# A PEER expert layer: 64 latent tokens instead of 32 fetched by gathers, 448 instead of 480 token columns in the dense expert products

## What is computed

```python
q = (xb @ w_pq).reshape(TOK_BLOCK, PEER_HEADS, 2, D_KEY_HALF)          # 8 heads, 2 halves
s = jnp.einsum('thcd,hcnd->thcn', q, sub_keys)                         # 128 keys a half
s1, i1 = lax.top_k(s[:, :, 0], 16); s2, i2 = lax.top_k(s[:, :, 1], 16)
top_s, pos = lax.top_k(s1[..., :, None] + s2[..., None, :], 16)        # 16 of 16 x 16
eidx = ...   # i1 * 128 + i2 of the chosen: 128 picks a token out of 16384 experts
g = jax.nn.softmax(top_s)
a = jax.nn.gelu(jnp.einsum('thkd,td->thk', u_exp[eidx], xb))
out = jnp.einsum('thk,thkd->td', g * a, v_exp[eidx])
```

## Time and profile before

| | us |
|---|---|
| three executions: median (lowest to highest) | 3987.83 (3984.5 to 3989.89) |
| profiled execution: its time | 3981.41 |
| profiled execution: span from first to last instruction | 3979.6 |
| u stage, layer 0 and 1 | 785.8 and 782.9 |
| v stage, layer 0 and 1 | 667.1 and 668.8 |

### The profile page before, as it was taken

How to read it: one execution, slowest core, us unless ns; L and a number is a source line. 1 busy time by engine, 2 the same in 40 slices (tenths; PEclk the granted TensorE clock), 3 DMA queues, 4 the chain that set the end, 5 groups by cost and what they waited for, 6 DMA issues and landing times.

```text
span 3979.6 us, 57585 instructions
## 1 busy us (share of the span) xinstructions
PE 3838.0 (96%) x21170; PEld 3355.6 (84%) x21170; DVE 2916.1 (73%) x4499; ACT 1673.6 (42%) x2920; POOL 2279.5 (57%) x1240
## 2 busy tenths in 40 slices
PE   7978899999999999999989989999999999999998
PEld 5756898888888888888879989888888888888886
DVE  4775218899875499999983320889987549999997
ACT  3265323556666422223231131355666643222322
POOL 1101224666666688888842222467666668888884
PEclk8999999999999999999999999999999999999999
DMA  5302324788888899999954312378888889999995
GB/s 209 129 2 81 127 85 138 264 281 305 302 302 308 313 342 317 330 319 327 335 181 175 117 54 90 131 257 285 300 302 300 311 314 341 314 327 322 321 333 185
DMA packets 396808, 972.44 MB, mean 244 GB/s; under 512 B 32160, under 2 KB 221344, under 8 KB 382880
## 3 DMA queue, kind: packets, MB, share of 16 engines
q1 hardware_dynamic: 301664, 630.72, 46.9%
q0 software_dynamic: 92160, 335.59, 22.7%
q10 hardware_dynamic: 2752, 3.21, 0.2%
HBM read 835.37 MB, written 133.96 MB: 244 GB/s over the span
## 4 chain that ended last, share of the span: by engine, by line
PE 57%; issue 26%; POOL 12%; DVE 4%; DMA 1%; DVEq 1%; ACT 0%; POOLq 0%; ACTq 0%
PE PS L775 30%; PE PS L763 18%; PE PS L565 5%; POOL SL L445 5%; POOL ROWS L452 4%; POOL SL L436 3%; PE PS L755 3%; DVE ROWS L1262 1%; PE PS L716 1%; DVE OH L1251 1%; DMA ROWS<-u_exp,EI 1%; DVE PO L1188 0%; DVE TS L1183 0%; DVE ABF L1218 0%; PE PS L548 0%
## 5 line engine op out<-in xcount | busy, mean ns | idle before, releaser
L445 POOL TENSOR_TENSOR SL<-RW,SH 128x1024 fp32r<-128x1024 f32 x512 | 1333.2, 2604 | 728.6 <-ACT SH L989 715.4
L989 ACT CAST SH<-RW 128x1024 fp32r<-128x1024 f32 x512 | 537.2, 1049 | 1430.3 <-PE PS L775 826.5
L763 PE MATMUL PS<-HH,SH 128*128 128x480 f32 x2048 | 799.6, 390 | 5.5 <-POOL SL L445 4.2
L775 PE MATMUL PS<-WH,SH 128*128 128x480 f32 x2048 | 777.0, 379 | 2.2 <-ACT GE L995 1.3
L763 PE MATMUL PS<-HH,SL 128*128 128x480 f32 x2048 | 776.5, 379 | 0.0
L763 PE MATMUL PS<-HL,SH 128*128 128x480 f32 x2048 | 776.3, 379 | 0.0
L775 PE MATMUL PS<-WH,SL 128*128 128x480 f32 x2048 | 775.2, 379 | 0.0
L775 PE MATMUL PS<-WL,SH 128*128 128x480 f32 x2048 | 775.1, 378 | 0.0
L436 POOL TENSOR_TENSOR SL<-RW,SH 128x1024 fp32r<-128x1024 f32 x84 | 202.6, 2416 | 808.3 <-ACT SH L820 808.3
L1312 DVE TENSOR_TENSOR WL<-GL,WH 128x480 fp32r<-128x480 f32 x256 | 558.6, 2182 | 20.6 <-ACT WH L1028 17.4
L1251 DVE TENSOR_TENSOR OH<-PS,PK 128x1024 f32<-128x1024 f32 x240 | 291.5, 1220 | 221.7 <-PE PS L755 207.7
(11 more groups left out here) (171 smaller groups left out, 5225.5 us busy)
## 6 DMA issues: line engine op xcount, KB each, us to landing
RW<-u_blk SPq DMA_DIRECT2D x256, 512.0 KB, 4.5
RW<-v_blk SPq DMA_DIRECT2D x256, 512.0 KB, 5.9
gate_acts<-GE SPq DMA_DIRECT2D x256, 240.0 KB, 3.2
router_weights<-GT SPq DMA_DIRECT2D x60, 1024.0 KB, 5.0
GB<-router_weights SPq DMA_DIRECT2D x32, 1920.0 KB, 14.5
GL<-gate_acts SPq DMA_DIRECT2D x256, 240.0 KB, 5.5
RW<-wstream SPq DMA_DIRECT2D x100, 512.0 KB, 4.3
AW<-wpairs SPq DMA_DIRECT2D x40, 1024.0 KB, 4.9
```

Source lines behind the costliest of these rows:

```text
L445: nc.gpsimd.tensor_tensor(SL[:, r % 2], RW[:, r % RAW], SH[:, r % 2].bitcast(F32), ALU.subtract).then_inc(raw_used, 1)
L763: last = mm(PS[:, n % 2, NG:NS], w[:, n % 2, j], a[:, j, NG:NS], start=(j == 0 and q == 0), stop=(j == DJ - 1 and q == 2))
L775: last = mm(PS[:, dj, NG:NS], w[:, k % 2, dj], a[:, k, NG:NS], start=start, stop=stop)
L989: nc.scalar.copy(SH[:, r % 2], RW[:, r % RAW]).then_inc(hi_done, 1)
```

## The change

`NG` goes from 32 to 64. From it follow `ND` 480 to 448 (columns of every dense product), `NQ` 120 to 112, `NTG` 30 to 28 (the groups of 16 tokens in the stores and loads of gate weights), `GQ` 4 to 2 picks side by side, `PG` 32 to 64 and `NPICK` 160 to 192. The table `PICK_AT` spreads the 32 more gathers of `u_exp` over the same blocks. `FOLD` gets 64 columns of its own in the constants.

```diff
-NG = 32
+NG = 64
 ND = NS - NG
 GQ = P // NG
 PG = PICKS // GQ
 NPICK = PICKS + PG
...
-PICK_AT = (_spread(20, 28, 9) + _spread(28, 45, 21) + _spread(45, 68, 36) + _spread(68, 91, 36)
-           + _spread(91, 127, NPICK - 102))
+PICK_AT = (_spread(20, 28, 11) + _spread(28, 45, 27) + _spread(45, 68, 42) + _spread(68, 91, 42)
+           + _spread(91, 127, NPICK - 122))
 VPICK_AT = _spread(2, NB_E, NPICK)
-C_MEAN, C_HEAD, C_SWAP, C_ID, C_IOTA, C_SEL, C_COS, C_SIN = 0, 128, 256, 384, 512, 640, 672, 1184
-C_ALL = 1696
+C_MEAN, C_HEAD, C_SWAP, C_ID, C_IOTA, C_SEL, C_FOLD, C_COS, C_SIN = 0, 128, 256, 384, 512, 640, 648, 712, 1224
+C_ALL = 1736
...
-    FOLD = CO[:, C_SEL:C_SEL + NG]
+    FOLD = CO[:, C_FOLD:C_FOLD + NG]
...
-    for s in range(32):
+    for s in range(2):
         c[:, C_SEL + s] = p % 32 == s
+    for t in range(NG):
+        c[:, C_FOLD + t] = p % NG == t
```

## The result

The changed kernel takes 4045.11 us (median of three, 4043.99 to 4049.84) against 3987.83. The ratio is 1.0148, with a 95% interval of 1.0125 to 1.0171: slower by 1.5%, above the forecast of 3990, above its own range (3965 to 4012) and above the whole range (3944 to 4030). Its profiled execution took 4049.84 us, with a span of 4048.0.

A forecast was written before the change was run, and what follows sets the result against it. TensorE was taken to bound, VectorE close behind and, in line with GpSimd, bounding the changed v stage. Per layer u −20 and v +21 gave +1, +2 in all: 3990 us, own range 3965 to 4012, whole range 3944 to 4030.

The forecast's parts named there:

- one line over VectorE and GpSimd: v stage: VectorE's operations with both inputs in SBUF and GpSimd's subtraction run one after the other, 5.06 us a block before.
- The v stage at 689 us, +21: v stage, per layer: serial work over VectorE and GpSimd was to take 5.38 us a block, up from about 668 us.
- The first way of the working: v stage: mean of blocks with one and two accumulations (4.72, 6.09), less 0.07 for narrower columns: 5.34 a block, 683 us.
- GpSimd's second gathers: v stage: gathers of 1.306 us each were to lie under VectorE's accumulations, so nothing was added for them.
- slack in the handing over: v stage: the 683 us sum had none between the engines, so 689 was taken.
- The second way: v stage: busy 636 plus short gaps make 656 us, plus 32 rows at 1.37, less 8.4: 691 us.
- a third party in the line: v stage: a block above 5.44 us would show something more in the serial line, most likely the gathers' issue.
- Rival 2: v stage, slower: VectorE and GpSimd serialise by whole instructions, 5.54 us a block, 709 a layer, 4030 in all; chance 0.24.
- Rival 1: v stage, faster: waiting inside VectorE is slack; 5.20 us a block gives 3944, TensorE's own pace 3800; chance 0.21.
- The u stage at 764.5, −20: u stage, per layer: stretches of 65.5, 188, 150, 145 and 216 us, against 784.4; VectorE bounds blocks 45 to 68.
- the 2 us for DMA in the last stretch: u stage, blocks 91 to 128: 12 more gathers raise DMA to 353 GB/s; 2 us added to TensorE's 213.6, making 216.
- The ends: Outside the two stages: fold with 64 columns, two pairs of small DMAs fewer, 40 constants more; about 1 us, counted as nothing.

## Why the prediction was wrong, point by point

- **TensorE bounds before, VectorE is close behind, and one line over VectorE and GpSimd decides the v stage.** Right, and shown from both sides: with one-input sums or with the subtraction off GpSimd, the stage falls to 638 to 651 us at about the same or more work for VectorE. TensorE's idle time in the v stage came to 7.5%, mostly released by `WL`, where 9% was forecast.
- **The v stage at 689 us, +21. This is the step that failed.** It measured 714.6, +46.7. The first way of the working, 5.34 a block or 683 us, is what two different runs without gather instructions took: 682.4 and 683.3 us. The prediction laid "GpSimd's second gathers" under VectorE's accumulations and put them at nothing. They cost 714.6 − 683 = 32 us a layer, 0.25 a block or 0.17 for each of the 192 gathers. GpSimd works in order, so its subtraction waits for the gather in front; a `GL` that begins in the meantime is not let through and ends behind the subtraction. Why it isn't let through stays open: beside a gather with no subtraction behind it on GpSimd, `GL` is not held at all. Nor is the price a fixed one, since with `GL` one block earlier and all gathers there two blocks took 10.48. That the sum of 10.67 was met to the last digit is thus in part luck, as a pattern of the same line is shorter.
- **The trace of before had it in view.** Both block lengths of the working, 4.72 and 6.09, were read where one gather stands in front of the subtraction. The next block has two. It holds one accumulation and takes 5.70 us (`GL` at 1711.67 to `GL` at 1717.37) instead of 4.72. `WL` begins 0.58 us before the subtraction and ends behind it:

```profile
1713.93 3.52 DVE L1312 TENSOR_TENSOR WL<-GL,WH 128x480 fp32r<-128x480 f32 x1 [0.24 <-ACT WH L1028]
1717.37 0.65 DVE L1306 TENSOR_TENSOR GL<-GL,GB 128x480 f32<-128x480 f32 x1
...
1712.87 1.63 POOL L452 DMA_INDIRECT ROWS<-v_exp,EI  x1 [0.31 <-issue]
1714.51 2.41 POOL L445 TENSOR_TENSOR SL<-RW,SH 128x1024 fp32r<-128x1024 f32 x1
```

  In layer 0 of the kernel before, a product or `WL` is passed over in this way 23 times. The line's 5.06 a block left these blocks out. They cost nothing then, as TensorE needed 5.21. The gathers of `v_exp` also took 1.306 in the mean, against 0.93 at their shortest, and no reason for that was asked.
- **Only 6 us were added for slack in the handing over**, where such a pattern costs 32. The second way, counting occupied time, gave 691 and missed it too: it priced a row at 1.37, and 1.78 was measured. The 0.07 us for the narrower `GL` and `WL` would be 0.09 by the rate that it names (0.644 us for 480 columns); 0.07 is what the trace shows (0.644 and 0.609 at their shortest, twice).
- **The sign was named.** A v stage above 5.44 was to mean "a third party in the line, most likely the gathers' issue". It came to 5.57 and 5.59, and the gathers' issue it was.
- **Rival 2** put the block at 5.54 and named the lost cover of the second gathers; 5.57 to 5.59 came. Its sum was of whole instructions, though, and hit the number by another way: the runs without gather instructions show the line's two-input operations at 5.33. It had 0.24 and should have been the forecast. Its 4030 for the whole lies below the result because its v stage is 5.6 a layer short and the u stage gave 5.3 less than forecast. The Trainium skill's rule on whole instructions (SBUF — State Buffer, section "Who interferes with whom") overshoots the line as measured, 5.54 against 5.34 without gathers. By these records it doesn't give the order of 1709.74 and 1710.12 either, where the later instruction went first. The same section says that descriptor generation was seen to be stalled by `tensor_copy` but not by `tensor_tensor`. The gathers here lasted from 0.93 to 1.95 us. They took 1.59 beside an accumulation, `WL` and `GL` in the changed kernel, but 0.94 beside an accumulation alone in the run with `GL` a block earlier. What sets their length is open.
- **Rival 1** (the waiting is slack) was wrong: the v stage got no faster in either layer.
- **The u stage at 764.5, −20.** It measured 769.8, −14.6. Blocks 0 to 13: 64.3 against 65.5 forecast. 13 to 45: 191.3 against 188. 45 to 68: 147.5 against 150. 68 to 91: 144.5 against 145. 91 to 128: 222.3 against 216. VectorE as the bound was right (145.44 of 147.50 in blocks 45 to 68). Blocks 13 to 45 gained nothing: VectorE was busy 176.49 us in layer 0 where the sum had 168.3, as the rows against `HTOK` went from 1.50 to 1.62 us each, and it still waited 12.1 us for rows. TensorE was idle for 14.7 us there, and its granted clock was 0.96 on average, against 1.00 before; what that cost was not taken apart. The mis-sized term is the 2 us for DMA in the last stretch, which cost 8.7. All of it stands in blocks 119 to 128, which took 55.3 us where 49.1 less 3.1 was to come, and 5.6 of it goes with the 12 gathers.
- **The ends cost nothing**: within 4 us of the profiled times.

## What to carry to other kernels

When two engines share a resource one instruction at a time, ask not how busy each is but what the sum is of all that stands in the line, and look at what stands in front of each of its members on its own engine: here a gather of about 1 us, which seems to touch nothing, delayed the subtraction behind it. Read the price of a block from blocks of every kind, also the odd one out. An engine at 95% whose instructions come in two lengths (0.64 and 2.85 us) is telling of such a line; the work then belongs where the turn is shortest, which was 1.22 us on VectorE against 2.4 on GpSimd. And a change that takes work off the bound is to be tried together with the one that clears the next bound: alone, each of the two was worth nothing or less, together they gave 2.0%.

## What the runs showed of the hardware

- In the changed kernel's order, gathers issued by GpSimd cost 32 us a v stage (0.17 for each of 192). Plain DMAs of the same size from SyncE cost nothing against no loads at all (683.3 and 682.4 us).
- A gather alone does not hold VectorE's two-input operations up: with the subtraction off GpSimd and the gathers kept, the longest `GL` of a stage was 0.628 us, against 3.298 in the changed kernel.
- Where a subtraction stands behind the gather on GpSimd, it goes ahead of a VectorE instruction whose record begins 0.36 to 0.39 us before it (1709.74 and 1710.12), 62 times in one stage.
- The line settles into a pattern of two blocks, 11.13 us in the changed kernel (89 and 93 of 126 distances in the two layers are 11.1) and 10.67 without the gathers (99 and 102 are 10.7). With `GL` a block earlier it reaches 10.48 with the gathers (49 and 49).
- The DMA engines moved 354 to 361 GB/s over a whole v stage or most of it, at a share of 0.99 to 1.01 (the runs with the subtraction on VectorE and with one-input sums).
